# Attention tiles of every second pair of heads taken from the shortest to the longest

## What is computed

```python
def forgetting_attention(q, k, v, logf):
    scale = d ** -0.5
    c = jnp.transpose(jnp.cumsum(logf, axis=1), (0, 2, 1))
    for i in range(lp // BLOCK):
        q0, kend = i * BLOCK, (i + 1) * BLOCK
        s = jnp.einsum('bqhd,bkhd->bhqk', q[:, q0:kend], k[:, :kend]) * scale
        s = s + c[:, :, q0:kend, None] - c[:, :, None, :kend]
        mask = (kpos[None, :kend] <= qpos[:, None]) & (kpos[None, :kend] >= PAD)
        p = jax.nn.softmax(jnp.where(mask[None, None], s, NEG_INF), axis=-1)
        outs.append(jnp.einsum('bhqk,bkhd->bqhd', p, v[:, :kend]))
```

## Time and profile before

| | us |
|---|---|
| median of three runs | 2883.32 |
| the profiled execution | 2876.48 |
| its span in the trace | 2874.7 |
| forgetting attention, from the first scores to the last result | 832.0 to 1313.3 |
| busy in the span: TensorE, VectorE, GpSimd, ScalarE | 2801.6, 1706.5, 1342.9, 622.4 |

### The profile page before, as it was taken

How to read it: one execution, slowest core, us unless ns; L and a number is a source line. 1 busy time by engine, 2 the same in 40 slices (tenths; PEclk the granted TensorE clock), 3 DMA queues, 4 the chain that set the end, 5 groups by cost and what they waited for, 6 DMA issues and landing times.

```text
span 2874.7 us, 40988 instructions
## 1 busy us (share of the span) xinstructions
PE 2801.6 (97%) x14586; PEld 2068.4 (72%) x14586; DVE 1706.5 (59%) x4617; ACT 622.4 (22%) x1276; POOL 1342.9 (47%) x1140
## 2 busy tenths in 40 slices
PE   8999999999999999999999999999999999999998
PEld 4488888888876566564555777878878777777765
DVE  6655656656347777773777445677677772333226
ACT  2222221210025555551111101101111111111115
POOL 3533434547731110111454345677667665565545
PEclk9999999999999999999999999999999999999999
DMA  6500010111121113015434468899889989999986
GB/s 223 188 6 17 15 46 1 30 29 31 37 72 38 62 34 130 29 34 210 172 133 162 127 231 242 251 284 278 272 281 285 283 282 293 305 301 314 313 251 256
DMA packets 192573, 470.52 MB, mean 164 GB/s; under 512 B 27384, under 2 KB 108104, under 8 KB 166632
## 3 DMA queue, kind: packets, MB, share of 16 engines
q1 hardware_dynamic: 145424, 347.63, 33.9%
q0 software_dynamic: 44640, 111.84, 16.8%
q10 hardware_dynamic: 2304, 8.39, 0.7%
HBM read 349.64 MB, written 118.11 MB: 163 GB/s over the span
## 4 chain that ended last, share of the span: by engine, by line
PE 39%; DMA 8%; POOL 3%; DVE 2%; issue 1%; ACT 0%; POOLq 0%; SPq 0%; DVEq 0%; ACTq 0%
PE ps L3057 17%; PE ps L2832 8%; DMA base_rows<-moe_yo,index 5%; PE ps L3005 4%; DMA moe_xg<-t_rows,index 3%; PE ps L2976 3%; PE ps L2888 2%; PE ps L2973 2%; DVE moe_xT L2133 1%; PE ps L2898 1%; POOL moe_xg L2559 1%; POOL base_rows L2580 1%; PE ps L2851 1%; POOL moe_fin L2641 1%; PE ps L2842 0%
## 5 line engine op out<-in xcount | busy, mean ns | idle before, releaser
L2559 POOL DMA_INDIRECT moe_xg<-t_rows,index x433 | 422.8, 976 | 166.5 <-issue 118.8
L3057 PEld LDWEIGHTS ps<-moe_xT,moe_wg 128*128 128x128 f32 x2048 | 353.6, 197 | 53.6 <-issue 29.6
L3057 PE MATMUL ps<-moe_xT,moe_wg 128*128 128x192 f32 (+22 forms) x2048 | 380.2, 339 | 8.7 <-DVE moe_hh L2033 8.6
L3057 PE MATMUL ps<-moe_xT,moe_wu 128*128 128x192 f32 (+22 forms) x2048 | 375.3, 336 | 0.0
L2133 DVE STREAM_TRANSPOSE moe_xT<-moe_xg 128x256 f32<-128x256 f32 x433 | 235.1, 609 | 209.6 <-DMA moe_xg<-t_rows,index 203.9
L2580 POOL DMA_INDIRECT base_rows<-moe_yo,index x100 | 228.9, 2289 | 279.2 <-DVE moe_yo L2147 98.8
L3057 PEld LDWEIGHTS ps<-moe_xT,moe_wu 128*128 128x128 f32 x2048 | 353.3, 196 | 4.3
L1342 POOL TENSOR_TENSOR fox_diag<-fox_c,fox_causal 128x128 f32<-128x128 f32 x128 | 55.8, 457 | 425.0 <-DVE fox_mx L1371 420.1
L2696 ACT ACTIVATE moe_sl<-ps 128x256 f32<-128x256 f32 (+19 forms) x144 | 49.8, 346 | 928.0 <-PE ps L3057 833.1
L1365 DVE CUSTOM_DVE_ANT_0 hT<-ps,fox_c 128x512 f32<-128x512 f32 (+7 forms) x320 | 166.6, 560 | 81.7 <-PE ps L1627 81.4
L2188 DVE SCALAR_TENSOR_TENSOR moe_yo<-ps,weight,moe_yo 128x512 f32<-128x512 f32 (+14 forms) x280 | 187.4, 741 | 27.7 <-ACT moe_yo L2719 27.7
(11 more groups left out here) (376 smaller groups left out, 5020.7 us busy)
## 6 DMA issues: line engine op xcount, KB each, us to landing
moe_wg<-in_we_gate SPq DMA_DIRECT2D x64, 1024.0 KB
moe_wu<-in_we_up SPq DMA_DIRECT2D x64, 1024.0 KB
moe_wd<-in_we_down SPq DMA_DIRECT2D x64, 1024.0 KB, 9.7
fox_c<-ck SPq DMA_DIRECT2D x8, 1032.0 KB, 8.8
emb_xin<-in_x SPq DMA_DIRECT2D x16, 512.0 KB, 4.3
h_rows<-emb_hr SPq DMA_DIRECT2D x16, 512.0 KB, 2.8
ret_w<-in_w_in SPq DMA_DIRECT2D x16, 512.0 KB, 6.5
moe_yt<-h_rows SPq DMA_DIRECT2D x16, 512.0 KB, 5.5
```

The source lines that it names most:

```text
L2559: pool.indirect_dma_start(out=xg[g % NXG][:, :], out_offset=None, in_=quarters, in_offset=bass.IndirectOffsetOnAxis(ap=route.index4[:, AT4 ...
L3057: ins = pe.matmul(out, w[:, c, f:FF:FC], xT[u][:, c, 0:n], start=(c == 0), stop=(c == DC - 1))
```

## The change

The list `order` lets pairs 1 and 3 go from t = 0 up to t = 7. Pair 0 and pair 2 stay as they were. So two short tiles meet (tile 0 of pair 0, tile 0 of pair 1, and the same with pairs 2 and 3), two long ones meet between pairs 1 and 2, and the last tile of the stage is tile 7 of pair 3. HALF is kept for the first tile alone. Tiles 0 and 1 of pairs 1 and 3 get one round more than they have groups, and tile 0 of pairs 0 and 2 has one round and not three. `TURN_AT` follows the long tiles.

At a tile with one group some calls change places. VectorE makes the reciprocals of a tile t = 0 in the last round of the tile before it, ahead of that tile's `finish`. In a tile with a single round it takes the biases ahead of all this, and TensorE turns the next tile behind the scores. ScalarE's `keep` of a tile t = 0 goes ahead of the copies for the next tile.

```diff
-        order = [(p, t) for p in range(PAIRS) for t in range(TILES - 1, -1, -1)]
+        order = [(p, t) for p in range(PAIRS) for t in (range(TILES) if p % 2 else range(TILES - 1, -1, -1))]
...
-        HALF = [6 if t == TILES - 1 else 0 for _, t in order]
+        HALF = [6 if n == 0 else 0 for n in range(NT)]
...
-        ROUNDS = [3 if t == 0 and n + 1 < NT else len(groups[n]) for n, (_, t) in enumerate(order)]
+        ROUNDS = [len(groups[n]) + (p % 2 and t < 2) for n, (p, t) in enumerate(order)]
...
-        TURN_AT = {TILES * p + x: TILES // 2 * p + x for p in range(PAIRS) for x in range(TILES // 2)}
+        TURN_AT = {TILES * p + x + TILES // 2 * (p % 2): TILES // 2 * p + x for p in range(PAIRS) for x in range(TILES // 2)}
... (VectorE)
+                    if i == ROUNDS[n] - 1 == 0:
+                        for m, u in scores_in[n, i]:
+                            bias(m, u)
                     if i == ROUNDS[n] - 1 and n + 1 < NT:
                         for s in groups[n + 1][0]:
                             back(n + 1, s)
-                    if i == (2 if HALF[n] else 0):
+                        if len(groups[n + 1]) == 1:
+                            inverse(n + 1)
+                    if i == (2 if HALF[n] else 0) and len(groups[n]) > 1:
                         inverse(n)
                     if i == len(groups[n]) - 1 and i >= 1:
                         finish(n)
-                    for m, u in scores_in[n, i]:
+                    for m, u in (scores_in[n, i] if ROUNDS[n] > 1 else []):
                         bias(m, u)
... (ScalarE)
+                    if len(groups[n]) == 1 and i == 0:
+                        keep(n)
...
-                    if i == spread_at[n]:
+                    if len(groups[n]) > 1 and i == spread_at[n]:
                         keep(n)
... (TensorE)
-                    if i == ROUNDS[n] - 1 and n + 1 < NT:
+                    if i == ROUNDS[n] - 1 >= 1 and n + 1 < NT:
                         for s in groups[n + 1][0]:
                             turn(n + 1, s)
...
+                    if i == ROUNDS[n] - 1 == 0 and n + 1 < NT:
+                        for s in groups[n + 1][0]:
+                            turn(n + 1, s)
```

## The result

The changed kernel takes 2895.89 us (median of 9 runs, 2891.03 to 2906.42), the kernel before in the same runs 2886.15 us (2882.12 to 2889.1): a ratio of 1.0038 with a 95% interval of 1.0027 to 1.005, so 8 to 14 us slower. A second set of runs gave 2894.65 to 2886.3, 1.0029 [1.0018, 1.004]. The forecast was 2887 us and no change that can be told; the time lies inside the range, near its upper end. In the table of the experiments, run 9's median has all twelve executions, and its ratio leaves out two of 3116 and 3259 us.

A forecast was written before the change was run, and what follows sets the result against it. TensorE, with its gaps in the attention, was taken as the bound; 12.9 us at meeting short tiles plus 9.2 in rising tiles minus 18.2 removed gave +3.9, so 2883.3 + 3.9 = 2887 us, range 2876 to 2897.

The forecast's parts named there:

- The reading of the bound: TensorE, busy 97% of the span, bounds the kernel; its attention gaps, 4.4 us at each change of pair, decide.
- The rival that the next stage would give the shift back: The next stage's first projection waits for something else, so the attention's end does not matter: 2883 us, 5%.
- What went away: Attention time removed: idle changes of pair, drawn-out scores, slow clock, last weighing's wait, half tiles and tail, 18.2 us in all.
- drawn-out scores, half tiles and tail: Savings in the attention: three lengthened score groups 1.1 us, fewer half-wise weighings 0.7, shorter chain at the stage's end 0.9.
- The short tiles' meeting: Where two short tiles meet, TensorE waits 6.05 us, plus 0.40 at tile 1; two places, 12.9 us.
- The rising tiles: Ahead of tiles 4, 5 and 7 TensorE waits for late exponentials: 3.75 us in pair 1, 5.45 in pair 3, 9.2 together.
- the ten waits of the walk: The TensorE waits summed by walking the queues in the attention, each of which may be off by half a microsecond.
- what comes in its place: Waits added in the attention: 12.9 us where short tiles meet and 9.2 us in rising tiles.
- The rival that named the clock: The clock falls behind five new TensorE gaps of 2 us or more, 1.7 us each: 2896 us; 21%, of which 19% slower.
- its point of decision: The clock rival decides from two slow places on, which takes the sum above 5.8 us.
- the forecast's own sign of being wrong: Among the signs of a wrong forecast: a slow clock at more than one of the attention's gaps.

The follow-up runs named there:

- run 9: The kernel before with only the sooner reciprocals and the engines' orders that go with them, old tile order and rounds: 2880.28 us, ratio 0.9971 to the kernel before.
- run 1: The changed kernel again, unaltered, for a second trace: 2894.65 us, ratio 1.0029 to the kernel before.
- run 7: The changed kernel with 110 more wait instructions on ScalarE ahead of the first exponentials: 2900.26 us, ratio 1.0042 to the kernel before.
- run 3: The changed kernel with three score units a round, not two, in tiles 2 to 6 of the rising pairs: 2899.0 us, ratio 1.0043 to the kernel before.
- run 8: The changed kernel with only the second pair rising, the fourth going downwards as before: 2884.52 us, ratio 0.9991 to the kernel before.
- run 2: The changed kernel with VectorE's `finish` of a short tile ahead of the next tile's biases and reciprocals: 2891.07 us, ratio 1.0023 to the kernel before.
- run 4: The changed kernel with both edits, those of run 2 and run 3: 2896.46 us, ratio 1.0037 to the kernel before.
- run 12: The kernel of run 9 again, unaltered, for a second trace: 2880.56 us, ratio 0.9975 to the kernel before.
- run 10: The kernel before with the rising order alone, three rounds for every shortest tile, reciprocals where they were: 2890.51 us, ratio 1.0011 to the kernel before.
- Run 11: The changed kernel with three rounds for tile 0 again and no additional round for tile 1: 2888.26 us, ratio 0.9997 to the kernel before.
- run 5: The kernel before again, unaltered, for a second trace: one execution, 2892.4 us.
- run 6: The kernel before with 18 more wait instructions on ScalarE ahead of the first exponentials: 2888.41 us, ratio 0.999 to the kernel before.

## Why the forecast was wrong

**The reading of the bound** was right. TensorE's gaps in the attention decide, and what the stage lost arrived behind it: the next stage's first product keeps its distance from the last weighing in every run (4.5 us behind a tile 7), and the ratios follow the stage's length to within some 3 us. The rival that the next stage would give the shift back falls.

**What went away** went as forecast: the 13.2 us of idle time at the old changes of pair, the last weighing's wait, and the work. Of the 7.9 us by which the stage grew, 8.9 are waits (22.69 for 13.8) and 1.7 are clock (3.4 for 1.7), which leaves -2.7 us, the 1.1 + 0.7 + 0.9 of drawn-out scores, half tiles and tail. The three are not told apart.

**A slip in the sum** is worth 0.4 us. The 0.40 us at tile 1 of the falling pair is counted at both meetings, but at the first it stands ahead of the windows of the earlier trace rows in both kernels. By the forecast's own terms the sum is 12.5 + 9.2 - 18.2 = +3.5 us, not +3.9.

**The short tiles' meeting** was priced at 6.05 us and took 5.03 and 5.48. Its chief wait, for `finish` behind biases and reciprocals, was walked to 2.15 us and is 2.14 at both places. The smaller ones were 0.8, 2.05 and 0.9 in the walk and 0.90, 2.04 and 0.40 at the second place; at the first, works at half clock used up part of the 2.05 (1.25 is left). The 0.15 us at a score unit of tile 3 did not come.

**The rising tiles** were priced at 9.2 us and took 11.8. The four kinds of wait that were named are each 0.2 to 0.25 us longer than walked (1.74 for 1.5, 0.92 for 0.7, 1.77 for 1.55, 3.50 for 3.25), and one was missed, 0.60 and 0.59 us at tile 5's last turn, for a copy by VectorE.

Waits in all: 21.7 us forecast from tile 1 of the first pair on (12.1 + 9.2 + the 0.40 of the second tile 1), 22.69 measured. So the ten waits of the walk were off by 1.0 us together.

**The clock is the step that failed.** "What goes away" counted the slow clock of one change, 1.7 us, and "what comes in its place" counted none, because two of three gaps of 1.97 us in the one trace had cost nothing. Measured: two stretches at the lower level, 1.7 us each, at the meetings. That is 3.4 us more than the sum had: 3.5 + 1.0 + 3.4 = 7.9, which the stage lost between the two profiled executions. Three traces of each order say the same. The changes of pair had lost 1.7, 3.4 and 5.1 us, 3.4 in the mean; the meetings lose 3.4, 3.4 and 8.6, 5.1 in the mean. So the clock adds 1.7 us where the forecast took 1.7 away. One trace with one in three was a thin base for either number.

In the three traces of the changed order, runs 1 and 7 among them, the lower level came at six of six meetings, and at all three meetings of the same form in runs 3 and 8; in three traces of the old order it came at five of nine changes. At the six it began within 2 us of the end of the 2.13 or 2.14 us gap five times, and once behind the gap of 2.04 us that follows (the scores at 1203.85 above). With `finish` first, where the gap of 2.04 or 2.05 us alone was left, it came at three of four (runs 2 and 4). Where the gaps were shortened it did not come: at none of six changes in runs 9 and 12, and at none of four meetings in runs 10 and 11. That ties it to the gaps; why a gap of 1.97 us draws it at one place and not at the next stays open.

The rival that named the clock had the mechanism and the price per place (1.7 us), and its point of decision, two places, is the number that came, as in the forecast's own sign of being wrong. It was wrong on the count: no trace shows the lower level at five places. The 3.50 us gap drew it in runs 1 and 7 and not in the first trace, and run 7 lost 10.3 us at three places, since the stretches at its meetings were two and three times as long. That the rival's 2896 us meets the median is chance: it had five places for two, on a base 2.8 us below the 2886.15 of the kernel before. The Trainium skill, TensorE: Matmul & The Clock Gate, section What's actually happening, was cited for a monitor that runs free of the kernel. The traces agree in that one program shows the lower level at different places from run to run (run 5 against the first trace).

**The base was a single profile.** The kernel before gave 2883.3 us in three runs and 2886.15 in nine, and its profile lacked a wait of ScalarE that all the other traces have (its two last silu waited for TensorE alone). That does not touch the forecast of the stage, but of the 18.0 us between the two spans 11.7 would have been blamed on the change without run 5. Against the medians the change costs 9.7 and 8.4 us; the stage gives 8.2 in the mean of three traces each (493.25, 494.04 and 497.04 against 485.31, 487.58 and 486.91), which lies in both intervals.

**What the forecast did not ask** was what each half does alone. The earlier trace rows had the answer: the 1.97 us wait for reciprocals stands at every old change, and the sooner reciprocals remove it without any new order. Priced by themselves they are three times 2.16 us and the clock behind them, 9.3 us measured; the rising order with its single rounds then costs 16 to 17 us on top of that. Run 11 splits these: 6 to 7 us are the rounds (493.25 and 494.04 against 487.07), about half of it waits and half clock, and 9.7 us the rising order (487.07 against 477.34), whose waits ahead of and in the long tiles are 11.8 us.

## What to carry to other kernels

Price the halves of a change apart before pricing the whole: here the sooner reciprocals alone were worth 9 us of the stage, the rising order gave 10 back by the waits of its long tiles, and the short tiles' fewer rounds another 6 to 7. In this kernel a gap of TensorE near two microseconds was followed by the lower clock, 1.7 us more, at five of nine places and at every meeting of the changed order. One trace doesn't tell how often: compare two or three before a slow stretch is written down as gone. And compare stages, not spans: a profile of before that happened to be fast can make a change look worse by more than the change is.

## What the runs showed that was not expected

One and the same kernel lost 2.4 to 5.8 us of clock in one stage in two traces. And the stretch ahead of the experts took 376.3 or 385.9 us in one program, with a wait of ScalarE that the records give to no engine of the core. In the second trace of before TensorE's products came singly meanwhile, with gaps in which it waited for nothing that the profile shows:

```profile
1686.36 0.38 PE L2888 MATMUL ps<-moe_xT,moe_sgu 128*128 128x256 f32 x1 [1.61 <-issue]
...
1689.89 3.08 PE L2888 MATMUL ps<-moe_xT,moe_sgu 128*128 128x256 f32 x6 [1.51 <-issue]
```

Runs 6 and 7 speak against the place of ScalarE's code as its cause; the cause stays open.
